# The end of routing in another order, in a decoder layer on one Trainium2 core

## What is computed

```python
def moe(h, w_router, b_router, w_up, b_up, w_down, b_down):
    logits = (x @ w_router + b_router)
    top_logit, top_idx = lax.top_k(logits, TOP_K)          # 4 of 32 experts
    top_w = jax.nn.softmax(top_logit, axis=-1)
    ...                                                    # rows sorted by expert, blocks of 128
    def expert_block(args):
        xe, e = args
        gu = xe @ w_up[e] + b_up[e]                        # 1024 -> 2048
        glu = jnp.minimum(gu[:, :D_FF], SWIGLU_LIMIT)
        lin = jnp.clip(gu[:, D_FF:], -SWIGLU_LIMIT, SWIGLU_LIMIT)
        act = glu * jax.nn.sigmoid(SWIGLU_ALPHA * glu) * (lin + 1.0)
        return act @ w_down[e] + b_down[e]                 # 1024 -> 1024
    ...                                                    # weighted by top_w, added to the tokens

x = x + moe(rmsnorm(x, norm_ffn), ...)
x = x + jax.nn.sigmoid(x @ w_ple_gate) * (p @ w_ple_proj)  # the embedding
```

## Time and profile before

| | |
|---|---|
| median of 3 runs | 1441.78 us (1441.73 to 1443.72) |
| the profiled execution | 1444.58 us, of which the profile's span is 1442.8 us |
| PE busy | 1410.2 us, 98% of the span |
| DVE busy | 1233.2 us, 85% |
| ACT busy | 928.4 us, 64% |
| POOL busy | 218.9 us, 15% |
| moved by DMA | 457.32 MB, mean 317 GB/s |

### The profile page before, as it was taken

The page is one execution under the profiler, slowest core; times in us unless marked ns, Lnnn a source line. Parts: engine busy times, 40 slices in busy tenths (PEclk is TensorE's granted clock), DMA queues, the critical chain, the costliest instruction groups (busy, mean ns, idle before and its releaser), DMA issues.

```text
span 1442.8 us, 19410 instructions
## 1 busy us (share of the span) xinstructions
PE 1410.2 (98%) x6551; PEld 1134.8 (79%) x6551; DVE 1233.2 (85%) x1007; ACT 928.4 (64%) x629; POOL 218.9 (15%) x130
## 2 busy tenths in 40 slices
PE   7999999999999999999999999999999999999997
PEld 5895557888888888888888888888888888888665
DVE  5742458999999999999999999999999999999885
ACT  4311236767777777777777777777777777777622
POOL 3131000221111111111111111111111111111100
PEclk9999989999999999999999999999999999999999
DMA  7114147999999999999999999999999999999661
GB/s 260 59 62 159 74 173 290 346 353 379 368 374 369 369 377 361 375 370 368 371 371 368 371 370 370 373 369 375 372 373 377 371 373 375 369 371 368 209 237 59
DMA packets 94169, 457.32 MB, mean 317 GB/s; under 512 B 13314, under 2 KB 14894, under 8 KB 60213
## 3 DMA queue, kind: packets, MB, share of 16 engines
q1 hardware_dynamic: 84255, 437.50, 79.7%
q0 software_dynamic: 9360, 17.85, 3.2%
q10 hardware_dynamic: 526, 1.60, 0.4%
HBM read 451.76 MB, written 21.58 MB: 328 GB/s over the span
## 4 chain that ended last, share of the span: by engine, by line
PE 94%; DVE 2%; issue 1%; ACT 1%; DMA 1%; POOL 0%; POOLq 0%; DVEq 0%; ACTq 0%
PE ps L1296 48%; PE ps L1305 24%; PE ps L1164 5%; PE ps L1445 2%; PE ps L1312 2%; PE ps L1284 2%; PE ps L1277 2%; PE ps L1099 1%; PE ps L1101 1%; PE ps L1106 1%; DVE resid L1935 1%; PE ps L1246 1%; PE ps L1044 1%; PE ps L1187 1%; PE ps L1041 1%
## 5 line engine op out<-in xcount | busy, mean ns | idle before, releaser
L1707 DVE TENSOR_TENSOR w_lo<-raw,w_hi 128x2048 fp32r<-128x2048 f32 x384 | 868.2, 2287 | 58.9 <-PE ps L1305 58.3
L878 ACT ACTIVATE w_hi<-raw 128x2048 fp32r<-128x2048 f32 x384 | 732.2, 1916 | 212.3 <-PE ps L1296 171.7
L1296 PE MATMUL ps<-w_hi,xT_hi 128*128 128x512 f32 x1024 | 278.4, 394 | 1.2 <-ACT xT_hi L897 1.1
L1296 PE MATMUL ps<-w_hi,xT_lo 128*128 128x512 f32 x1024 | 275.2, 391 | 0.1
L1305 PE MATMUL ps<-w_lo,xT_hi 128*128 128x512 f32 x1024 | 274.7, 390 | 0.0
L1296 PEld LDWEIGHTS ps<-w_hi,xT_lo 128*128 128x128 f32 x1024 | 192.6, 188 | 41.8 <-DVE xT_lo L1763 0.5
L1305 PEld LDWEIGHTS ps<-w_lo,xT_hi 128*128 128x128 f32 x1024 | 192.8, 188 | 40.3
L1296 PEld LDWEIGHTS ps<-w_hi,xT_hi 128*128 128x128 f32 x1024 | 190.4, 189 | 40.1 <-ACT xT_hi L897 1.4
L729 POOL DMA_INDIRECT expert_rows<-y_rows,scatter_col x32 | 145.6, 4551 | 402.8 <-ACT y_rows L911 402.8
L1296 PE MATMUL ps<-w_hi,aT_hi 128*128 128x512 f32 x512 | 139.9, 395 | 0.0
L1296 PE MATMUL ps<-w_hi,aT_lo 128*128 128x512 f32 x512 | 136.9, 389 | 0.0
(11 more groups left out here) (276 smaller groups left out, 1172.0 us busy)
## 6 DMA issues: line engine op xcount, KB each, us to landing
raw<-in_w_up_dram SPq DMA_DIRECT2D x256, 1024.0 KB, 6.5
raw<-in_w_down_dram SPq DMA_DIRECT2D x128, 1024.0 KB, 7.5
raw<-in_w_ple_gate_dram SPq DMA_DIRECT2D x4, 1024.0 KB, 5.4
yk<-expert_rows SPq DMA_DIRECT2D x4, 1024.0 KB, 7.0
raw<-expert_rows SPq DMA_DIRECT2D x4, 1024.0 KB, 6.5
resid<-in_x_prompt_dram SPq DMA_DIRECT2D x4, 512.0 KB, 7.8
w_v_sb<-in_w_in_dram SPq DMA_DIRECT2D x2, 1024.0 KB, 8.2
w_z_sb<-in_w_in_dram SPq DMA_DIRECT2D x2, 1024.0 KB, 13.1
```

The lines of the kernel that those rows point to most:

```text
L878: act.activation(w_hi[:, s % SPLIT, :], raw[:, s % RING, :], ACT.Copy).then_inc(s_hi, 1)
L1296: mm = pe.matmul(out[:, c:c + 512], (xh, xl)[xs], w_hi[:, s % SPLIT, base + c:base + c + 512], start=(fresh and xs == 0 and base == 0), st ...
L1707: dve.tensor_tensor(w_lo[:, s % SPLIT, :], raw[:, s % RING, :], w_hi[:, s % SPLIT, :].bitcast(F32), ALU.subtract).then_inc(s_lo, 1)
```

## The change

Five things move, and nothing is computed otherwise.

- PE makes the first half of the embedding before the last ranks, into banks 4 and 5 of PSUM (before: banks 0 and 1, those of `gu`). The second half follows the bias products of expert 0, which no longer wait for ACT's copy of the embedding.
- DVE reads the slots, makes `code_of` and `token_of`, copies the counts, and does `lo_part(0, 0)`; only then come the overflow counts and the gates' first steps. The one-hot for expert 0 is made before the loop over tiles.
- The gates' reduction and copies go behind `lo_part(0, 1)`.
- PE's gate transposes go behind the up products of expert 0. ACT's copy of them goes into step 0 behind the second `hi_part`, and DVE's subtraction behind its third `lo_part`. The down products of step 0 wait for it.
- `up_bias` is cut into halves: the first waits for `glu`, the second for `lin`.

```diff
@@ -309,7 +309,7 @@
         rank_bank = ps[:, 7, :]
         count_cols = ps[:, 6, 2 * E:3 * E]
         slot_cols = ps[:, 2, 0:E]
-        ple_banks = ps[:, 0:2, :]
+        ple_banks = ps[:, 4:6, :]
         gates_banks = ps[:, 4:6, :]
 
         def out_banks(i):
@@ -370,6 +370,7 @@
         s_rkp = sem("ranks_summed")
         s_rkd = sem("ranks_read")
         s_cntp = sem("counts_summed")
+        s_cntd = sem("counts_read")
         s_pTp = sem("p_transposed")
         s_pTd = sem("pT_copied")
         s_slp = sem("slots_summed")
@@ -888,8 +889,6 @@
             hi_part(0, 2)
             act.wait_ge(s_ple0p, 1)
             act.activation(ple0[:], ple_banks.rearrange("p a n -> p (a n)"), ACT.Copy).then_inc(s_ple0d, 1)
-            act.wait_ge(s_gTp, 1)
-            act.activation(gatesT[:], gates_banks.rearrange("p a n -> p (a n)")[:, 0:T], ACT.Copy).then_inc(s_gthi, 1)
 
 
             def xT_high(u):
@@ -915,6 +914,9 @@
                     hi_part(J, UP_CHUNKS + x)
                     if x == 0 and first:
                         swish(0)
+                    if x == 1 and first:
+                        act.wait_ge(s_gTp, 1)
+                        act.activation(gatesT[:], gates_banks.rearrange("p a n -> p (a n)")[:, 0:T], ACT.Copy).then_inc(s_gthi, 1)
                     if x == 2 and not first:
                         y_out(J - 1, STEP_CHUNKS * J + UP_CHUNKS)
                     if x == 4:
@@ -1228,10 +1230,20 @@
             for k in range(KP):
                 mm = pe.transpose(ps[:, 3, k * NS:(k + 1) * NS], p_sb[0:NS, LAST, k * P:(k + 1) * P], ident[0:NS, 0:NS])
             mm.then_inc(s_pTp, 1)
+            def embedding(out, t, bs=(0, 1)):
+                pe.wait_ge(ld["ple"], 16)
+                for b in bs:
+                    for k in range(KP):
+                        mm = pe.matmul(out[0:NT[t], b, :], pT[:, k, t * P:t * P + NT[t]], w_proj_sb[:, k, b * 512:(b + 1) * 512],
+                                       start=(k == 0), stop=(k == KP - 1))
+                return mm
+
             for t in range(LAST - 1):
                 slots(t)
             router(LAST)
             slots(LAST - 1)
+            pe.wait_ge(s_pTd, 2)
+            embedding(ple_banks, 0, bs=(0,))
             ranks(LAST)
             pe.wait_ge(s_lgd, TT)
             for t in range(TT):
@@ -1239,23 +1251,13 @@
             mm.then_inc(s_cntp, 1)
             slots(LAST)
 
-            def embedding(out, t):
-                pe.wait_ge(ld["ple"], 16)
-                for b in range(2):
-                    for k in range(KP):
-                        mm = pe.matmul(out[0:NT[t], b, :], pT[:, k, t * P:t * P + NT[t]], w_proj_sb[:, k, b * 512:(b + 1) * 512],
-                                       start=(k == 0), stop=(k == KP - 1))
-                return mm
-
-            pe.wait_ge(s_pTd, 2)
-            embedding(ple_banks, 0).then_inc(s_ple0p, 1)
-            pe.wait_ge(s_gates, 1)
-            pe.wait_ge(s_h2d, TT)
-            for t in range(TT):
-                mm = pe.transpose(gates_banks[:, t // 4, (t % 4) * P:(t % 4) * P + NT[t]],
-                                  gates[0:NT[t], t].rearrange("p g e -> p (g e)"), ident[0:NT[t], 0:NT[t]])
-            mm.then_inc(s_gTp, 1)
-
+            def gates_transposes():
+                pe.wait_ge(s_gates, 1)
+                pe.wait_ge(s_ple0d, 1)
+                for t in range(TT):
+                    mm = pe.transpose(gates_banks[:, t // 4, (t % 4) * P:(t % 4) * P + NT[t]],
+                                      gates[0:NT[t], t].rearrange("p g e -> p (g e)"), ident[0:NT[t], 0:NT[t]])
+                mm.then_inc(s_gTp, 1)
 
             def over_slots():
 
@@ -1306,18 +1308,20 @@
                                        start=False, stop=last and k == len(parts) - 1, skip_group_check=True)
                 mm.then_inc(s_lused, 1)
 
-            def up_bias(u):
-                pe.wait_ge(s_oh, u + 1)
-                for c in range(0, 2 * FF, 512):
+            def up_bias(u, half):
+                if half == 0:
+                    pe.wait_ge(s_oh, u + 1)
+                for c in range(half * FF, (half + 1) * FF, 512):
                     pe.matmul(gu[:, c:c + 512], oh_up[:], bias_hl[:, c:c + 512], start=True, stop=False, skip_group_check=True)
 
             def up_start(u, late_low=False):
                 pe.wait_ge(s_xhi, u + 1)
                 if not late_low:
                     pe.wait_ge(s_xlo, u + 1)
+                pe.wait_ge(s_glu, u)
+                up_bias(u, 0)
                 pe.wait_ge(s_lin, u)
-                pe.wait_ge(s_glu, u)
-                up_bias(u)
+                up_bias(u, 1)
 
             def up_args(c):
                 return gu, [(xT_hi[:, c, :], xT_lo[:, c, :], 0, 2 * FF)]
@@ -1358,6 +1362,8 @@
                         over_slots()
                 for c in range(DN_CHUNKS):
                     if c == 0:
+                        if first:
+                            pe.wait_ge(s_gTd, 1)
                         if over:
                             pe.wait_ge(s_overd, 1)
                         dn_start(J)
@@ -1370,8 +1376,10 @@
 
             pe.wait_ge(s_bias, 4)
             pe.wait_ge(s_sld, 1)
-            pe.wait_ge(s_ple0d, 1)
-            up_bias(0)
+            up_bias(0, 0)
+            up_bias(0, 1)
+            embedding(ple_banks, 0, bs=(1,)).then_inc(s_ple0p, 1)
+            pe.wait_ge(s_cntd, 1)
             x_transposes(0)
             pe.wait_ge(s_xhi, 1)
             for c in range(UP_CHUNKS):
@@ -1381,6 +1389,7 @@
                 if c == UP_CHUNKS - 2:
                     x_transposes(1)
             up_lo(0, UP_CHUNKS - 1, UP_CHUNKS - 1)
+            gates_transposes()
             step(0, first=True)
             step(1, over=True)
             pe.wait_ge(s_route, 1)
@@ -1675,6 +1684,9 @@
             dve.tensor_copy(ones_r[:], ones[:])
             dve.tensor_copy(before_r[:], before[:])
             dve.tensor_tensor(mask0[:, 0, :], ones[:, 0:E], ones[:, 0:E], ALU.subtract)
+            link(dve.tensor_copy(cur_expert[:], expert_iota[:, 0:1]))
+            dve.tensor_scalar(oh_up[:], bias_row[:, 0:1].to_broadcast([P, P]), cur_expert[:, 0:1], None,
+                              ALU.is_equal).then_inc(s_oh, 1)
             for i in range(TT):
                 if i > 0:
                     logits_top(i - 1)
@@ -1721,8 +1733,14 @@
                                   over_pos[:, :, k:k + 1].to_broadcast([P, TT, P]), ALU.is_equal).then_inc(s_overpicks, 1)
 
             ranks(LAST)
+            dve.wait_ge(s_slp, 1)
+            dve.tensor_scalar(code_of[:, 0:E], slot_cols, float(NO_ROW), None, ALU.add).then_inc(s_sld, 1)
+            dve.wait_ge(s_sld, 1)
+            dve.tensor_scalar(token_of[:, 0:E], code_of[:, 0:E], 2, None, ALU.logical_shift_right).then_inc(s_code, 1)
             dve.wait_ge(s_cntp, 1)
-            link(dve.tensor_copy(count[:], count_cols))
+            dve.tensor_copy(count[:], count_cols).then_inc(s_cntd, 1)
+            lo_part(0, 0)
+            dve.wait_ge(s_cntd, 1)
             dve.tensor_scalar(over_depth[:], pos[:], float(2 * P), None, ALU.is_ge)
             link(dve.tensor_scalar(over[:], count[:], float(P + 1), None, ALU.is_ge))
             for m in range(2, TT):
@@ -1736,29 +1754,13 @@
             dve.scalar_tensor_tensor(out=over_pos[:], in0=over_depth[:], scalar=float(-P), in1=pos[:], op0=ALU.mult, op1=ALU.add)
             link(dve.tensor_tensor(over_from[:], over_end[:], over[:], ALU.subtract))
             dve.tensor_scalar(over_pos[:], over_pos[:], float(P), None, ALU.subtract)
-            dve.wait_ge(s_slp, 1)
-            dve.tensor_scalar(code_of[:, 0:E], slot_cols, float(NO_ROW), None, ALU.add).then_inc(s_sld, 1)
-            dve.wait_ge(s_sld, 1)
-            dve.tensor_scalar(token_of[:, 0:E], code_of[:, 0:E], 2, None, ALU.logical_shift_right).then_inc(s_code, 1)
-
             dve.memset(gates[:, :, 3, :], 0.0)
             dve.wait_ge(s_exp, TT)
             link(dve.reciprocal(exp_rcp[:], exp_sum[:]))
             link(dve.tensor_tensor(topw[:], exps[:], exp_rcp[:].rearrange("p (t o) -> p t o", o=1).to_broadcast([P, TT, TOPK]),
                                    ALU.mult))
             link(dve.tensor_tensor(route_tmp[:], chosen[:], by_choice(topw[:]).to_broadcast([P, TT, TOPK, E]), ALU.mult))
-            link(dve.tensor_reduce(gates[:, :, 0, :], route_tmp[:].rearrange("p t k e -> p t e k"), AX.X, ALU.add))
-            for g in range(1, 3):
-                ins = dve.tensor_copy(gates[:, :, g, :], gates[:, :, 0, :])
-            ins.then_inc(s_gates, 1)
             dve.tensor_copy(block_expert[:, 0:E], expert_iota[:])
-            link(dve.tensor_copy(cur_expert[:], expert_iota[:, 0:1]))
-            dve.tensor_scalar(oh_up[:], bias_row[:, 0:1].to_broadcast([P, P]), cur_expert[:, 0:1], None,
-                              ALU.is_equal).then_inc(s_oh, 1)
-            lo_part(0, 0)
-            dve.wait_ge(s_gthi, 1)
```

(11 more changed lines are left out.)

## The result

The changed kernel took 1450.24 us (median of 5 runs, 1446.74 to 1452.08) against 1441.78 us for the kernel before beside it (5 runs, 1439.57 to 1443.72): a ratio of 1.0049, 95% interval 1.0037 to 1.0061. By the medians it is slower by 8.5 us, by the means of the five runs (1449.54 and 1442.10) by 7.4 us, where 2.6 us was forecast.

What follows compares the result with a forecast made beforehand. PE was taken as bound in the main loop, with one chain setting its start at 215.4 us. Transposes +1.4, clock +1.1 and smaller edits +0.1 gave +2.6 us on 1441.8: 1444.4 us, range 1440.8 to 1447.2.

Steps and rivals of the forecast that it cites:

- The mechanism: Before expert 0's row transposes: the moved subtraction holds the first gather's issue, PE waits for the gather, its clock falls.
- Rival 1: First gather's issue isn't held by the subtraction; transposes start 0.5 us earlier than before, 1441.4 us; chance 0.2.
- Issue's start: POOL issues the first gather 1.55 us later, at 206.35: slots 2.5 us later, codes ahead of counts give back 0.95.
- Hold: The moved subtraction on DVE holds the first gather's issue until 209.3, 0.9 us after the subtraction's end.
- My rule: A POOL indirect DMA's issue ends about 0.9 us after the last DVE operation reading two operands from SBUF.
- Landing: Gather lands 3.3 to 5.2 us after its issue, near 213.5, beside a weight load; row transposes put at +1.4 us.
- The clock: PE idle around the row transposes brings low clock; 3.4 us of products at half speed, +1.1 us, between 0 and 1.7.
- Rival 2: Low clock comes after 244.5, where PE has no gap; costs 1.7 to 3.4 us, 1446.9 us; chance 0.15.
- The gates' subtraction: DVE's 0.72 us gates subtraction in step 0, in a stretch without a gap: +0.1 us, between 0 and 0.7.
- The other small edits: One-hot, gates' reduction and copies, gate transposes, ACT's gates copy and split bias halves were each put at 0 us.

Runs made afterwards that it cites:

- The short ones: Changed kernel with lo_part(0, 0) later and four 512-column additions in its place, one operand in PSUM or both in SBUF: 1445.69 and 1445.94 us.
- first profile: Profiled execution of the changed kernel, nothing edited, the fastest of its five runs: 1446.74 us.
- second profile: Profile of the changed kernel run again unedited, standing for its usual run: 1450.73 us.

## Why the prediction was wrong

- *The mechanism was right, the sum too small.* The issue was held (3.18 us; forecast 2.5 to 3.3), PE waited for the gather's DMA, the clock was low between 212 and 220. Rival 1 (not held) fell at once.
- *Issue's start.* Forecast +1.55 us, measured +1.0 and +0.8 from the router. The half embedding was priced at 3.35 us; it took 2.98 and overlapped the ranks' products and their wait, so the slots end 1.9 and 1.8 us later, not 2.5.
- *Hold.* Forecast end 0.9 us behind the subtraction, measured 1.19. My rule named the last DVE operation with two SBUF operands. The short ones show that it is the one under way, at least for this gather; the scatters that the rule came from don't fit that either (see Open). For one 2.28 us subtraction both give the same, so this error cost nothing here, but it hid the cheap remedy.
- *Landing.* Between 3.3 and 5.2 us, 4.2 taken; measured 4.9 and 4.7. The load in its way is worth 1.5 us. T0 therefore came 2.0 and 1.7 us later, not 1.4: mis-sized by 0.3 to 0.6. (The transposes forecast at 213.5 were 1.5 us late; the sum took 1.4.)
- *The clock, the step that failed.* I took +1.1 us, bounded by 1.7, on the view that one stretch of 3.4 us at half clock would meet the idle PE. The fall that met it lasted 6.8 us (210.6 to 217.4) in the first profile and 10.2 us (211.8 to 222.0) in the second, and T0 to T1 took 1.9 and 3.2 us more, both beyond the bound. The bound came from a single 2.5 us gap of before with products at full clock ahead of it; this gap is 3.7 to 4.0 us, with half-clock work ahead of it and transposes behind it. Filling it gave back 3.6 us in the mean of the timed runs, and 1.8 us from T0 to T1 in the profiles.
- *Rival 2, the late fall*, got 0.15. It is there in the second profile (249.03), +1.6 us, just under its price of 1.7 to 3.4, and not in the first. Over all profiles it came in 5 of the 14 with the late parts and in none of the 3 without them or with the gate transposes moved (T1 to A0 of 16.2 us against 14.6 to 14.7): a chance of .15 was low. Means of 7.4 and 7.9 us over ten timed runs lie nearer the second profile's 6.6 than the first's 4.6. The rest isn't traced to a stage; the profile of before is itself of a run some 2 us above that kernel's mean.
- *The gates' subtraction.* Taken +0.1, measured +0.7, the upper bound, where the clock didn't fall late. The lead of 0.6 to 0.9 us that I read off didn't absorb it.
- *The other small edits* cost nothing that the profiles show.

In all: 1.4 + 1.1 + 0.1 forecast, 2.0 + 1.9 + 0.7 in the first profile, 1.7 + 3.2 + 1.6 in the second. Three terms were bounded one by one, and I took middles, though one thing (PE idle before narrow work) drives two of them upward together.

Open: why the scatters of before are held across several subtractions where this gather isn't held across four short ones. Their subtractions are 2.29 us long, and no kernel here shortened those, but length alone isn't the answer: beside the scatter held for 11.81 us (282.08 to 293.89) operations of 0.82 us with two SBUF operands (`over_picks`, four of them) stand between the long ones, and it wasn't let in behind them. Open too: whether the gates' subtraction is all of the 0.7; and what sets the whole of the spread between runs, which goes with the mean granted clock (0.988 in the changed kernel, 0.992 before).

## What to carry to other kernels

Before moving a long two-operand vector operation next to a GpSimd DMA issue, look at what waits for that DMA, or cut the operation into parts: four of 512 columns let this gather's issue end after 1.58 us where one of 2048 held it for 3.18. For a scatter that isn't shown. Judge two moves on one chain together: each alone was harmless because the other's place gave cover, and only both opened the idle time. Price idle TensorE time ahead of dense work at its length plus what the products behind it lose to the clock, and keep the widest measured loss as the bound.

## What the runs showed of the hardware

- A gather's issue gets in between short DVE operations with two SBUF operands (1.58 us beside 512-column ones of 0.68 us each, 1.32 us with one operand in PSUM), and is held by a single one of 2048 columns (3.18 us; 1.32 us with one operand in PSUM). Whenever the first gather was held, its issue ended 1.19 to 1.20 us after the operation that was under way at its start.
- The granted clock fell during 3.7 and 4.0 us of idle time of PE and stayed low into products that kept PE busy (5.63 of 6.00 us at 0.50): for 6.8 us in one profile of the same kernel, for 10.2 us in the other. Useless products in the gap made the kernel 3.6 us faster.
- One 1 MB weight load beside the gather of 128 rows moved its landing from 3.3 to 4.7 and 4.9 us after the end of its issue.
